# Latent values projected behind the attention's first batch of scores, with the last weight split and the mLSTM tile splits of that place moved to later batches

## The chip, the cores and the metric

The kernel runs on one core of a Trainium2 chip. The time is device microseconds for the whole program. The time before is 1668.84 us, the median of three runs (1668.3 to 1670.27). The profile is of one further execution, which took 1666.45 us.

## The reference

Two layers (DEPTH = 2) of a decoder trunk over 512 tokens of width 1024, float32. Each layer mixes tokens by three head groups fed by one input projection, then does cross-attention into 256 memory tokens and a SwiGLU block, each between RMSNorms. The change is in the token mixing:

```
h = rms_norm(x, norm_mix_pre[l])
(c_q, c_kv, k_rope, ml_q, ..., sw_v) = split(h @ w_in[l])
y_a = mla_mixer(...)          # A: latent attention, 8 heads, causal
y_b = mlstm_mixer(...)        # B: matrix memory, 4 heads, chunks of 128
y_c = dilated_swa_mixer(...)  # C: dilated window attention, 4 heads
y = concatenate([y_a, y_b, y_c]) @ w_out[l]

# inside A:
q  = rms_norm(c_q) @ w_uq     # 8 heads of 64 + 32 (rotary)
kv = rms_norm(c_kv) @ w_ukv   # 8 heads of 64 keys + 64 values
s  = (q . k + q_rope . k_pe) * scale, causal;  out = softmax(s) @ v
```

## The kernel before

**Precision.** Every projection is done as three matmuls on numbers split into a rounded half and a residual: hi*hi, hi*lo, lo*hi (`three`, lines 555 to 557). Weights stream from memory in units of 128 x 1024 floats through a ring of four slots (`RING`). ScalarE makes the rounded half of a unit (`split_unit`, line 990), VectorE the residual (`lo_to`, line 1362), and both calls stand at written places of each engine's program (`split_until(n)`, `lo_until(n)`: make all units below n). A slot is split again once TensorE has used it up (`unit_used`); SyncE loads the next unit once the residual is made (`split_lo`).

**Order.** There is no scheduler: each engine runs a program in a written order and waits for semaphores. ScalarE, VectorE and TensorE each pass through the same numbered steps. `tile_plan` lists the tiles that a projection makes, in the order of use, with the engine that empties each from its bank. In the stretch at hand all go through two banks in turn (`dense`), so a tile waits until the one two places ahead of it has been emptied (`wait_emptied(..., use - 2)`).

**The mLSTM steps.** Nine steps (`ML_STEPS`) work through two head pairs of four key blocks. In step s TensorE makes the scores of block s and the numerators of block s - 1, then a share of the list `BETWEEN` (`do_between`): here 53 items of three matmuls (a few of one): three sliding-window tiles (`sw`) of eight items, four rotations (`rot`), the key (`key`), eight query tiles (`uq`) of two, four key tiles (`uk`) and four value tiles (`uv`). Item i belongs to step i * 9 // 53, so the steps hold 5 or 6 items. ScalarE in step s makes the exponential weights of block s + 1 (`ml_weights`), and on some steps a part of a pair's end: absolute values (`ml_sums`), the reciprocal (`ml_invert`), the rounded output (`ml_output_hi`). VectorE makes the products (`ml_probs`) and on some steps `ml_diagonals`, `ml_denominators`, `ml_finish`, `ml_output_lo`. After that each of the two empties the tiles that the step has completed, and splits the units that are free then. Value tile m is emptied by ScalarE into `v_mla[:, m, :]`. The last step holds k_nope tiles 2 and 3 and the four value tiles; behind it both engines split the unit that takes the value weights' slot (the output projection's fourth).

**The attention batches.** Latent and window heads go in six pairs of three batches (`BATCH`: query blocks 0 and 1, block 2, block 3), 18 in all. At step s TensorE makes the scores of batch s (`pair_scores`), then the output of a pair whose three batches are copied (`pair_out`), then transposes the probabilities of batch s - 2 (`pair_transposes`). VectorE masks and takes the row minimum (`pair_mask`, line 1674) and copies one head's transposes (`pair_copy`, line 1685), ScalarE makes the exponentials (`pair_exp`, line 1245) and copies the other head's (`pair_copy`, line 1234). Even batches have their scores in banks 2 and 3, odd ones in the dense banks, so batch 1 waits for the last value tile to be emptied. Batch s waits for batch s - 2 to be masked. The transposes of batch t wait, for each head, until the copy of batch t - 1 is made. `ml_finish(1)` and `ml_output_lo(1)` of VectorE and `ml_output_hi(1)` of ScalarE stand at batches 0, 1 and 1.

The first output (`pair_out(0)`, line 837) is the first reader of `v_mla`. The output projection starts after the last batch and is the first to read the unit split above.

Of the kernel before, what the change touches and what calls it, by code (L numbers as in the profile page):

```python
# [20 lines left out]
P = 128  # L21
# [89 lines left out]
def tile_plan():  # L111


    plan, uses = {}, []

    def add(name, sub, engine):
        plan.setdefault(name, []).append((len(uses), sub))
        uses.append((sub, engine))

    def whole(name, u0, n, engine="act", order=range(KT)):  # L120
        for m in range(n):
            add(name, [(u0 + m, k * P) for k in order], engine)

    def query(t):

        add("uq", [(U_UQ + t // 4, ((t % 4) * 2 + k) * P) for k in range(2)], "dve" if t % 2 else "act")

    def rotation():
        add("rot", [], "dve")

    whole("in", U_IN, IN_FM, "dve")

    whole("sw", U_SW, 2, "dve")
    rotation()
    whole("sw", U_SW + 2, 1, "dve")
    rotation()
    whole("sw", U_SW + 3, 1, "dve")
    rotation()
    add("key", [], "act")
    query(0)  # L140
    rotation()
    for t in range(1, MLA_HEADS):
        query(t)
    for m in range(4):
        add("uk", [(U_UKV, m * P)], "act")
    for _ in range(TB):
        add("uv", [(U_UKV, SEQ)], "act")
    whole("out", U_OUT, KT, order=OUT_ORDER)
    whole("xk", U_XK, KT)
    whole("xq", U_XQ, KT)  # L150
    whole("xo", U_XO, KT)
    for m in range(KT):
        add("down", [(U_DOWN + (m * FT + k) // KT, (m * FT + k) % KT * P) for k in range(FT)], "act")
    return plan, uses
# [17 lines left out]
def emptied(use):  # L172
# [6 lines left out]
ML_PAIRS = ML_HEADS // 2  # L179
ML_UNITS = ML_PAIRS * TB  # L180
ML_STEPS = ML_UNITS + 1
BETWEEN = [(name, m, k) for use in range(PLAN["sw"][1][0], PLAN["out"][0][0])
           for name in ("sw", "rot", "key", "uq", "uk", "uv") for m, (at, sub) in enumerate(PLAN[name]) if at == use
           for k in range(max(len(sub), 1))]


# [83 lines left out]
def build(nc, x_in, mem_in, w_in, g_in, c_in, out):  # L270
    with ExitStack() as ctx:
# [231 lines left out]
        with nc.Block() as block:  # L503
# [46 lines left out]
            def _(pe):  # L550
                pe.wait_ge(fixed_set, 2)
                for layer in range(DEPTH):
# [134 lines left out]
                    def do_between(step):  # L687

                        for name, m, k in between(step):
                            use = use_of(name, m)  # L690
                            if name == "sw":
                                project_step("sw", m, k, tiles(h_hi), tiles(h_lo))
                            elif name == "uq":
                                if m == 0:
                                    after_norm("q")(k)
                                project_step("uq", m, k, tiles(cq_hi), tiles(cq_lo))
                            elif name == "uk":
                                if m == 0:
                                    after_norm("kv")(k)
                                project_step("uk", m, k, lambda k: ckv_hi[:, :], lambda k: ckv_lo[:, :])  # L700
                            elif name == "uv":
                                s, t = slot(layer, U_UKV), slice(m * P, (m + 1) * P)
                                wait_emptied(pe, layer, use - 2)
                                mm = three(dense[use % 2][:, :], ckv_hi[:, t], ckv_lo[:, t], w_hi[:, s, SEQ:2 * SEQ],
                                           w_lo[:, s, SEQ:2 * SEQ], True, True)
                                mm.then_inc(unit_used if ends_unit(use) else tile_done, 1)
                            elif name == "key":
                                wait_emptied(pe, layer, use - 2)
                                pe.wait_ge(key_scaled, count(key_scaled, layer, 1))
                                pe.matmul(dense[use % 2][:, :], const(C_KEY), c_tile(MISC), start=True, stop=True)\  # L710
                                  .then_inc(tile_done, 1)
                            else:

                                wait_emptied(pe, layer, use - 2)
                                wait_emptied(pe, layer, use_of("sw", m))
                                pe.matmul(dense[use % 2][:, :], const(C_ROT), sw_qk[:, m, :], start=True, stop=True)\
                                  .then_inc(tile_done, 1)
# [45 lines left out]
                    def attention(a, heads, probs, klen, emit_scores, emit_out, before_last):  # L763
# [3 lines left out]
                        for u in range(n_units + LAG + OUT_LAG):  # L767
# [16 lines left out]
                            if w >= 0 and w % TB == TB - 1:  # L784
                                pe.wait_ge(a["copied"], count(a["copied"], layer, w + 1))
                                emit_out(w // TB)

                    def pair_scores(c):

                        for i in range(2):  # L790
                            if c == 0 and i == 0:
                                wait_emptied(pe, layer, use_of("uq", MLA_HEADS - 1))
                                wait_emptied(pe, layer, use_of("uk", 3))
                                pe.wait_ge(ml_prob, count(ml_prob, layer, 2 * ML_UNITS))
                                pe.wait_ge(roped, count(roped, layer, 4))
                            if c == 1 and i == 0:
                                wait_emptied(pe, layer, use_of("uv", TB - 1))
                            if c >= 2:
                                pe.wait_ge(mix_at["masked"], count(mix_at["masked"], layer, batch_end(c - 2, i)))
                        parts = [mix_head(2 * (c // BATCHES) + i)["parts"] for i in range(2)]  # L800
                        last = len(parts[0]) - 1
                        for qb, at, u in batch_blocks(c):
                            n = causal_len(qb)
                            for part in range(last + 1):
                                for i in range(2):
                                    q, k = parts[i][part]
                                    mm = pe.matmul(score_bank(c, i)[:, at:at + n], q[:, qb * P:n], k[:, 0:n],  # L807
                                                   start=(part == 0), stop=(part == last))
                                    if part == last:
                                        mm.then_inc(mix_at["scored"], 1)  # L810
# [53 lines left out]
                    for s in range(PAIR_STEPS + PAIR_LAG + 1):  # L864
                        if s < PAIR_STEPS:
                            pair_scores(s)
                        t = s - PAIR_LAG
                        if t == PAIR_STEPS:
                            for j in range(KT - 2):
                                out_step(0, j)  # L870
                        if t >= 1 and t % BATCHES == 0:
                            pair_out(t // BATCHES - 1)
                        if 0 <= t < PAIR_STEPS:
                            pair_transposes(t)
# [103 lines left out]
            def _(act):  # L978
# [32 lines left out]
                for layer in range(DEPTH):  # L1011
# [144 lines left out]
                    def ml_output_hi(pair):  # L1156
# [3 lines left out]
                        act.activation(h_hi[:, 4 + pair, :], o_gate[:, pair, :], ACT.Copy).then_inc(ml_hi, 1)  # L1160

                    mix_tiles = {"key": lambda m: k_pe[:, :], "uq": lambda m: q_nope[:, m // 2, :],
                                 "uk": lambda m: k_nope[:, m, :], "uv": lambda m: v_mla[:, m, :]}

                    ml_floors(0)
                    ml_weights(0)
# [70 lines left out]
                    def pair_exp(c):  # L1237

                        for qb, at, u0 in batch_blocks(c):
                            n = causal_len(qb)  # L1240
                            for i in range(2):
                                u = u0 + i
                                act.wait_ge(mix_at["masked"], count(mix_at["masked"], layer, u + 1))
                                p = batch_probs(c, i)[:, at:at + n]
                                act.activation(p, p, ACT.Exp, scale=-1.0, bias=stat[:, 0, u:u + 1],  # L1245
                                               accum_out=stat[:, 1, u:u + 1]).then_inc(mix_at["exped"], 1)

                    for s in range(PAIR_STEPS + PAIR_LAG + 1):
                        t = s - PAIR_LAG
# [3 lines left out]
                            pair_copy(t)  # L1253
                        if s < PAIR_STEPS:
                            pair_exp(s)
                        if s == 1:
                            ml_output_hi(1)
                        if t == PAIR_STEPS:
                            pair_hi(MIX_PAIRS - 1)

# [67 lines left out]
            def _(dve):  # L1328
# [57 lines left out]
                for layer in range(DEPTH):  # L1386
# [275 lines left out]
                    def pair_mask(c):  # L1662

                        hd = mix_head(2 * (c // BATCHES))
                        for qb, at, u0 in batch_blocks(c):
                            n = causal_len(qb)
                            for i in range(2):
# [3 lines left out]
                                if 2 * c + i >= PAIR_PROBS and at == 0:  # L1671
# [3 lines left out]
                                    batch_probs(c, i)[:, at:at + n], score_bank(c, i)[:, at:at + n],  # L1675
                                    const(hd["mask"] + SEQ - n, n), -hd["scale"], 3e38, ALU.add, ALU.min,
                                    stat[:, 0, u:u + 1]), mix_at["masked"])

                    def pair_copy(c):

# [6 lines left out]
                    for s in range(PAIR_STEPS + PAIR_LAG + 2):  # L1687
                        if s < PAIR_STEPS:
                            pair_mask(s)
                        if s == 0:  # L1690
                            ml_finish(1)
                        if s == 1:
                            ml_output_lo(1)
                        if 0 <= s - PAIR_LAG < PAIR_STEPS:
                            pair_copy(s - PAIR_LAG)
                        if s >= 1 and s % BATCHES == 0 and s <= PAIR_STEPS:
# [227 lines left out]
```

## Time and profile before

| | |
|---|---|
| median of three runs | 1668.84 us |
| profiled execution, its own time | 1666.45 us |
| its span, first to last instruction | 1664.7 us |
| TensorE busy | 1582.2 us (95%) |
| VectorE busy | 902.6 us (54%) |
| ScalarE busy | 724.4 us (44%) |
| mean granted TensorE clock | 0.996 |

Busy shares are of the span. A matmul's record overlaps the next one's, so TensorE's pace is read from the distance between starts, and its idle time from the brackets behind a row, which give the idle time just before the instruction and what ended it. The mLSTM steps of layer 0 begin near 110 us, the attention batches run from 170.95 to about 243 us; in layer 1 both come some 819 us later. Lines are those of the kernel before.

### The profile page before, as it was taken

What the parts mean: (1) busy time and instruction counts of PE and PEld (TensorE: products, weight loads), DVE (VectorE), ACT (ScalarE), POOL (GpSimd) and SP (SyncE); (2) the same over time, 40 slices, a digit from 0 to 9 for tenths busy, and PEclk for the clock granted to TensorE, in tenths of its full rate; (3) what the DMA queues carried; (4) which work ended last, traced back from release to release, by engine and by line L of the source; (5) the groups of instructions that cost most, each with busy time, mean ns of one, the idle gap of its engine ahead of it and who ended that gap; (6) DMA issues with size and microseconds to landing.
All of it is one profiled execution on the core that took longest, in us unless ns stands there. A gap on an engine that the chain in (4) does not pass through costs nothing.

```text
span 1664.7 us, 19239 instructions
## 1 busy us (share of the span) xinstructions
PE 1582.2 (95%) x7420; PEld 1238.2 (74%) x7420; DVE 902.6 (54%) x1396; ACT 724.4 (44%) x1224; POOL 20.1 (1%) x26
## 2 busy tenths in 40 slices
PE   6999899999999999999989989998999999999995
PEld 5776568777768888888767655787867788888884
DVE  5766645854375555532287666458254655555223
ACT  5544645534444444432245356455254444444221
POOL 0000010000000000000000001000000000000000
PEclk9999999999999999999999999999999999999998
DMA  5321003530212333333212200235302133333321
GB/s 224 108 73 42 1 25 128 165 114 26 89 55 97 102 101 98 99 109 101 89 47 93 89 13 1 89 101 165 101 15 100 51 102 101 102 101 104 111 65 50
DMA packets 38538, 143.47 MB, mean 86 GB/s; under 512 B 4272, under 2 KB 4400, under 8 KB 37936
## 3 DMA queue, kind: packets, MB, share of 16 engines
q1 hardware_dynamic: 38448, 142.25, 26.0%
q8 instruction: 59, 0.97, 0.2%
q14 instruction: 31, 0.25, 0.0%
HBM read 140.13 MB, written 2.10 MB: 85 GB/s over the span
## 4 chain that ended last, share of the span: by engine, by line
PE 87%; DVE 7%; ACT 3%; issue 2%; DMA 0%; SPq 0%; DVEq 0%; ACTq 0%
PE bank L555 25%; PE bank L557 25%; PE bank L556 25%; PE bank L807 2%; PE bank L837 2%; PE bank L915 2%; PE bank L905 1%; PE bank L824 1%; PE bank L747 1%; DVE x L1437 1%; DVE tn_x L1402 1%; PE bank L736 1%; PE bank L602 1%; DVE acc L1343 1%; DVE h_lo L1407 1%
## 5 line engine op out<-in xcount | busy, mean ns | idle before, releaser
L555 PE MATMUL bank<-h_hi,w_hi 128*128 128x512 f32 x1312 | 522.5, 398 | 27.9 <-DVE h_lo L1349 16.8
L1362 DVE TENSOR_TENSOR w_lo<-raw,w_hi 128x1024 fp32r<-128x1024 f32 x254 | 310.2, 1225 | 427.6 <-ACT w_hi L990 425.6
L556 PE MATMUL bank<-h_lo,w_hi 128*128 128x512 f32 x1312 | 512.5, 391 | 0.0
L557 PE MATMUL bank<-h_hi,w_lo 128*128 128x512 f32 x1312 | 512.5, 391 | 0.0
L990 ACT ACTIVATE w_hi<-raw 128x1024 fp32r<-128x1024 f32 x254 | 266.0, 1051 | 186.3 <-PE bank L557 176.0
L555 PEld LDWEIGHTS bank<-h_hi,w_hi 128*128 128x128 f32 x1312 | 247.1, 188 | 97.5 <-issue 25.0
L556 PEld LDWEIGHTS bank<-h_lo,w_hi 128*128 128x128 f32 x1312 | 247.3, 189 | 52.4 <-issue 2.9
L557 PEld LDWEIGHTS bank<-h_hi,w_lo 128*128 128x128 f32 x1312 | 247.1, 188 | 52.5
L556 PE MATMUL bank<-a_lo,w_hi 128*128 128x512 f32 x352 | 136.9, 389 | 0.0
L557 PE MATMUL bank<-a_hi,w_lo 128*128 128x512 f32 x352 | 136.9, 389 | 0.0
L555 PE MATMUL bank<-a_hi,w_hi 128*128 128x512 f32 x352 | 136.9, 389 | 0.0
L1343 DVE TENSOR_TENSOR acc<-acc,sq 128x512 f32<-128x512 f32 x84 | 58.0, 690 | 86.7 <-ACT sq L1009 85.6
L1318 ACT ACTIVATE a_hi<-sq 128x512 fp32r<-128x512 f32 x44 | 27.8, 632 | 140.7 <-DVE sq L1768 140.7
L1009 ACT ACTIVATE sq<-bank 128x512 f32<-128x512 f32 x48 | 28.6, 596 | 125.9 <-PE bank L557 125.9
L556 PEld LDWEIGHTS bank<-a_lo,w_hi 128*128 128x128 f32 x352 | 66.1, 188 | 13.8
L557 PEld LDWEIGHTS bank<-a_hi,w_lo 128*128 128x128 f32 x352 | 66.1, 188 | 13.8
L555 PEld LDWEIGHTS bank<-a_hi,w_hi 128*128 128x128 f32 x352 | 66.1, 188 | 13.5
L1313 ACT ACTIVATE acc<-sq 128x512 f32<-128x512 f32 x44 | 27.8, 632 | 110.0 <-DVE sq L1761 110.0
L555 PE MATMUL bank<-m_hi,w_hi 128*128 128x256 f32 x128 | 38.0, 297 | 5.6 <-DVE w_lo L1362 5.0
L1001 ACT ACTIVATE h_hi<-x,gains 128x512 fp32r<-128x512 f32 x32 | 23.0, 720 | 35.3 <-DVE x L1437 33.2
L1685 DVE COPY pt_mix<-bank 128x384 f32<-128x384 f32 (+1 forms) x36 | 21.7, 601 | 30.9 <-PE bank L824 30.1
L1245 ACT ACTIVATE p_mix<-p_mix,stat 128x128 f32<-128x128 f32 (+2 forms) x72 | 35.7, 499 | 3.9 <-DVE stat L1674 3.9
(210 smaller groups left out, 1850.9 us busy)
## 6 DMA issues: line engine op xcount, KB each, us to landing
raw<-w_in SPq DMA_DIRECT2D x254, 512.0 KB, 3.6
x<-x_in SPq DMA_DIRECT2D x4, 512.0 KB, 8.2
mem<-mem_in SPq DMA_DIRECT2D x2, 1024.0 KB, 4.9
out<-x SPq DMA_DIRECT2D x4, 512.0 KB, 2.6
consts<-c_in SPq DMA_DIRECT2D x1, 1600.0 KB, 12.9
mem_sq<-mem_in SPq DMA_DIRECT2D x1, 1024.0 KB, 6.0
gains<-g_in SPq DMA_DIRECT2D x1, 80.0 KB, 3.4
```

Source lines behind the costliest of these rows:

```text
L555: pe.matmul(out_ap, l_hi, r_hi, start=start, stop=False)
L556: pe.matmul(out_ap, l_hi, r_lo, start=False, stop=False)
L557: return pe.matmul(out_ap, l_lo, r_hi, start=False, stop=stop)
L807: mm = pe.matmul(score_bank(c, i)[:, at:at + n], q[:, qb * P:n], k[:, 0:n], start=(part == 0), stop=(part == last))
L837: mm = pe.matmul(outs[pair % 2][64 * i:64 * i + 64, q0 * P:(q0 + rows.stop - rows.start) * P], mix_head(2 * pair + i)["v"](kb), pt_mix[:, ...
L915: mm = pe.matmul(outs[c][:, :], v_x[:, kb, col:col + P], pt_x[:, head % 2, kb, :], start=(kb == 0), stop=(kb == 1))
L990: act.activation(w_hi[:, s, :], raw[:, s, :], ACT.Copy).then_inc(split_hi, 1)
L1009: act.activation(sq[:, c % 2, 0:width], src, ACT.Square).then_inc(squared, 1)
L1245: act.activation(p, p, ACT.Exp, scale=-1.0, bias=stat[:, 0, u:u + 1], accum_out=stat[:, 1, u:u + 1]).then_inc(mix_at["exped"], 1)
L1313: done(act.activation(sig, gate_up, ACT.Exp, scale=-1.0), act_step)
L1343: ins = dve.tensor_tensor(acc[:, :], acc[:, :], sq[:, c % 2, :], ALU.add)
L1362: dve.tensor_tensor(w_lo[:, s, :], raw[:, s, :], w_hi[:, s, :].bitcast(F32), ALU.subtract)\
```

## The change

The value tiles leave the between list, which now has 49 items over nine steps. TensorE makes them in a new function, `value_tiles`, right behind the scores of batch 0. Tiles 0 and 2 are emptied by ScalarE inside `pair_exp(0)`, tiles 1 and 3 by VectorE inside `pair_mask(0)`, each behind the query block of the same place. Batch 1 waits for tiles 2 and 3. On ScalarE `ml_output_hi(1)` moves from batch 1 to batch 2, and the split of the unit in the value weights' slot to batch 3. On VectorE `ml_output_lo(1)` and the residual of that unit stand at batch 3, between its masks and its copy.

```diff
--- before.py
+++ after.py
@@ -143,8 +143,8 @@
         query(t)
     for m in range(4):
         add("uk", [(U_UKV, m * P)], "act")
-    for _ in range(TB):
-        add("uv", [(U_UKV, SEQ)], "act")
+    for t in range(TB):
+        add("uv", [(U_UKV, SEQ)], "dve" if t % 2 else "act")
     whole("out", U_OUT, KT, order=OUT_ORDER)
     whole("xk", U_XK, KT)
     whole("xq", U_XQ, KT)
@@ -179,8 +179,8 @@
 ML_PAIRS = ML_HEADS // 2
 ML_UNITS = ML_PAIRS * TB
 ML_STEPS = ML_UNITS + 1
-BETWEEN = [(name, m, k) for use in range(PLAN["sw"][1][0], PLAN["out"][0][0])
-           for name in ("sw", "rot", "key", "uq", "uk", "uv") for m, (at, sub) in enumerate(PLAN[name]) if at == use
+BETWEEN = [(name, m, k) for use in range(PLAN["sw"][1][0], PLAN["uv"][0][0])
+           for name in ("sw", "rot", "key", "uq", "uk") for m, (at, sub) in enumerate(PLAN[name]) if at == use
            for k in range(max(len(sub), 1))]
 
 
@@ -698,12 +698,6 @@
                                 if m == 0:
                                     after_norm("kv")(k)
                                 project_step("uk", m, k, lambda k: ckv_hi[:, :], lambda k: ckv_lo[:, :])
-                            elif name == "uv":
-                                s, t = slot(layer, U_UKV), slice(m * P, (m + 1) * P)
-                                wait_emptied(pe, layer, use - 2)
-                                mm = three(dense[use % 2][:, :], ckv_hi[:, t], ckv_lo[:, t], w_hi[:, s, SEQ:2 * SEQ],
-                                           w_lo[:, s, SEQ:2 * SEQ], True, True)
-                                mm.then_inc(unit_used if ends_unit(use) else tile_done, 1)
                             elif name == "key":
                                 wait_emptied(pe, layer, use - 2)
                                 pe.wait_ge(key_scaled, count(key_scaled, layer, 1))
@@ -785,6 +779,16 @@
                                 pe.wait_ge(a["copied"], count(a["copied"], layer, w + 1))
                                 emit_out(w // TB)
 
+                    def value_tiles():
+
+                        s = slot(layer, U_UKV)
+                        for m in range(TB):
+                            use, t = use_of("uv", m), slice(m * P, (m + 1) * P)
+                            wait_emptied(pe, layer, use - 2)
+                            mm = three(dense[use % 2][:, :], ckv_hi[:, t], ckv_lo[:, t], w_hi[:, s, SEQ:2 * SEQ],
+                                       w_lo[:, s, SEQ:2 * SEQ], True, True)
+                            mm.then_inc(unit_used if ends_unit(use) else tile_done, 1)
+
                     def pair_scores(c):
 
                         for i in range(2):
@@ -794,7 +798,8 @@
                                 pe.wait_ge(ml_prob, count(ml_prob, layer, 2 * ML_UNITS))
                                 pe.wait_ge(roped, count(roped, layer, 4))
                             if c == 1 and i == 0:
-                                wait_emptied(pe, layer, use_of("uv", TB - 1))
+                                for m in range(TB - 2, TB):
+                                    wait_emptied(pe, layer, use_of("uv", m))
                             if c >= 2:
                                 pe.wait_ge(mix_at["masked"], count(mix_at["masked"], layer, batch_end(c - 2, i)))
                         parts = [mix_head(2 * (c // BATCHES) + i)["parts"] for i in range(2)]
@@ -864,6 +869,8 @@
                     for s in range(PAIR_STEPS + PAIR_LAG + 1):
                         if s < PAIR_STEPS:
                             pair_scores(s)
+                        if s == 0:
+                            value_tiles()
                         t = s - PAIR_LAG
                         if t == PAIR_STEPS:
                             for j in range(KT - 2):
@@ -1160,7 +1167,7 @@
                         act.activation(h_hi[:, 4 + pair, :], o_gate[:, pair, :], ACT.Copy).then_inc(ml_hi, 1)
 
                     mix_tiles = {"key": lambda m: k_pe[:, :], "uq": lambda m: q_nope[:, m // 2, :],
-                                 "uk": lambda m: k_nope[:, m, :], "uv": lambda m: v_mla[:, m, :]}
+                                 "uk": lambda m: k_nope[:, m, :]}
 
                     ml_floors(0)
                     ml_weights(0)
@@ -1244,6 +1251,8 @@
                                 p = batch_probs(c, i)[:, at:at + n]
                                 act.activation(p, p, ACT.Exp, scale=-1.0, bias=stat[:, 0, u:u + 1],
                                                accum_out=stat[:, 1, u:u + 1]).then_inc(mix_at["exped"], 1)
+                            if c == 0:
+                                empty("uv", 2 * qb, v_mla[:, 2 * qb, :])
 
                     for s in range(PAIR_STEPS + PAIR_LAG + 1):
                         t = s - PAIR_LAG
@@ -1253,8 +1262,10 @@
                             pair_copy(t)
                         if s < PAIR_STEPS:
                             pair_exp(s)
-                        if s == 1:
+                        if s == 2:
                             ml_output_hi(1)
+                        if s == 3:
+                            split_until(U_OUT + RING)
                         if t == PAIR_STEPS:
                             pair_hi(MIX_PAIRS - 1)
 
@@ -1675,6 +1686,10 @@
                                     batch_probs(c, i)[:, at:at + n], score_bank(c, i)[:, at:at + n],
                                     const(hd["mask"] + SEQ - n, n), -hd["scale"], 3e38, ALU.add, ALU.min,
                                     stat[:, 0, u:u + 1]), mix_at["masked"])
+                            if c == 0:
+                                m = 2 * qb + 1
+                                wait_tile(dve, layer, use_of("uv", m))
+                                done(dve.tensor_copy(v_mla[:, m, :], dense[use_of("uv", m) % 2][:, :]), emptied_dve)
 
                     def pair_copy(c):
 
@@ -1689,8 +1704,9 @@
                             pair_mask(s)
                         if s == 0:
                             ml_finish(1)
-                        if s == 1:
+                        if s == 3:
                             ml_output_lo(1)
+                            lo_until(U_OUT + RING)
                         if 0 <= s - PAIR_LAG < PAIR_STEPS:
                             pair_copy(s - PAIR_LAG)
                         if s >= 1 and s % BATCHES == 0 and s <= PAIR_STEPS:
```

## Rows read from the trace of the kernel before

**Rows 1.** The page's chain that ended last, share of the span by engine.

```profile
PE 87%; DVE 7%; ACT 3%; issue 2%; DMA 0%; SPq 0%; DVEq 0%; ACTq 0%
```

**Rows 2.** TensorE's waits, 110 to 190 us: line, releaser, total us, times, longest.

```profile
PE bank L807 <- DVE stat L1674: 2.1, 1, 2.1
PE bank L824 <- DVE pt_mix L1685: 2.0, 1, 2.0
PE bank L555 <- ACT q_nope L1188: 1.5, 1, 1.5
PE bank L710 <- DVE sw_qk L1424: 0.9, 1, 0.9
PE bank L555 <- ACT k_nope L1188: 0.8, 1, 0.8
PE bank L555 <- issue: 0.8, 1, 0.8
```

**Rows 3.** Busy time by engine (PE, PEld, DVE, ACT, POOL), granted clock, DMA: layer 1.

```profile
969.76:1006.86 37.10, 32.22 (x169) 21.25 (x167) 22.41 (x52) 23.11 (x54) 0.00 (x0) 1.00 0.00 1
```

**Rows 4.** TensorE in time order: start us, length us, line, operands, [idle before].

```profile
150.30 0.40 PE L555 MATMUL bank<-cq_hi,w_hi 128*128 128x512 f32 x1
...
150.99 0.39 PE L555 MATMUL bank<-cq_hi,w_hi 128*128 128x512 f32 x1
...
164.85 0.61 PE L747 MATMUL bank<-w_ml,ml_v 128*128 128x128 f32 x4
...
170.95 0.49 PE L807 MATMUL bank<-k_nope,q_nope 64*128 64x128 f32 x4
...
175.87 1.13 PE L807 MATMUL bank<-k_nope,q_nope 64*128 64x512 f32 x4 [2.05 <-DVE stat L1674]
...
177.79 0.87 PE L824 MATMUL bank<-consts,p_mix 128*128 128x128 f32 x6
...
187.52 2.38 PE L837 MATMUL bank<-pt_mix,v_mla 128*64 128x384 f32 x20
```

**Rows 5.** ScalarE in time order, layer 0.

```profile
146.58 0.40 ACT L1133 ACTIVATE w_ml<-sq,acol 128x128 f32<-128x128 f32 x1 [3.94 <-PE bank L747]
...
148.87 0.58 ACT L1188 ACTIVATE q_nope<-bank 128x512 f32<-128x512 f32 x1
...
165.76 1.21 ACT L1146 ACTIVATE conv_in<-bank 64x512 f32<-64x512 f32 x2
...
171.74 1.06 ACT L990 ACTIVATE w_hi<-raw 128x1024 fp32r<-128x1024 f32 x1
...
181.20 0.72 ACT L1245 ACTIVATE tn_mix<-tn_mix,stat 128x512 f32<-128x512 f32 x1 [1.19 <-DVE stat L1674]
...
182.65 0.47 ACT L1234 ACTIVATE pt_mix<-bank 128x384 f32<-128x384 f32 x1
...
184.28 0.49 ACT L1245 ACTIVATE p_mix<-p_mix,stat 128x256 f32<-128x256 f32 x1
```

**Rows 6.** VectorE in time order, layer 0.

```profile
165.62 1.40 DVE L1573 COPY rstd<-bank 64x512 f32<-64x512 f32 x2
...
172.90 1.22 DVE L1362 TENSOR_TENSOR w_lo<-raw,w_hi 128x1024 fp32r<-128x1024 f32 x1 [5.10 <-ACT w_hi L990]
...
175.29 0.42 DVE L1674 CUSTOM_DVE_ANT_0 p_mix<-bank,consts 128x256 f32<-128x256 f32 x1
...
181.93 0.56 DVE L1685 COPY pt_mix<-bank 128x384 f32<-128x384 f32 x1
```

**Rows 7.** TensorE at pauses of the span, and busy time and clock past its end.

```profile
16.53 0.79 PE L555 MATMUL bank<-h_hi,w_hi 128*128 128x512 f32 x1 [2.51 <-DVE w_lo L1362]
...
21.81 0.51 PE L555 MATMUL bank<-h_hi,w_hi 128*128 128x512 f32 x1
...
466.68 0.47 PE L555 MATMUL bank<-h_hi,w_hi 128*128 128x512 f32 x1 [2.14 <-DVE h_lo L1349]
...
1650.00:1655.00 5.00, 0.00 (x0) 0.00 (x0) 3.97 (x7) 0.84 (x2) 0.00 (x0) 0.52 0.00 0
```

## What the change will do to the time: the prediction

> **What bounds the kernel now.** I read the chain of waits first: TensorE carries 87% of the chain that ended last, VectorE 7%, ScalarE 3% [rows 1]. So a change pays only where TensorE stands still. Next I listed TensorE's waits over 110 to 190 us of layer 0, the stretch in which the mLSTM steps with their in-between tiles end and the first attention batches begin. Six pauses matter: 0.9 (for the last sliding-window tile), 0.8 (for the third rotation to be emptied; the view says "issue"), 1.5 (for ScalarE's first query tile), 0.8 (for a k_nope copy), 2.1 (batch 2 of scores waits for batch 0 to be masked) and 2.0 (the second half of the transposes of batch 1 waits for VectorE's copy of batch 0), 8.1 us in all [rows 2]. Layer 1 repeats it: from query 1's second half to the first output 37.1 us, at a granted clock of 1.00 [rows 3], against 187.52 - 150.30 = 37.2 in layer 0 [rows 4]. So one layer is worked out and doubled. No pause outside this stretch is touched.
>
> The unit of measure is one in-between item of three 512-column matmuls: 150.30 to 150.99, 0.69 us [rows 4]. An item behind a pause takes 0.1 longer.
>
> **Part 1, four value items leave the mLSTM steps.** The in-between list shrinks from 53 to 49 items for nine steps, so each boundary slides: eight steps had 47 items ahead of the last, now 43. Nothing is saved by this alone; 4 x 0.69 = 2.75 us stand behind batch 0 instead. What changes is which copy each step waits for. I followed all three engines in their program order, with durations of before.
>
> Removed: key and query 0 now come in step 5, behind numerators 4, not ahead of them. The waits of 0.9 and 0.8 go, because VectorE works off its copy while TensorE does the mLSTM part. Query 1 no longer waits 1.5 for query 0.
> Put in their place: the third sliding-window tile starts on a copy that stands behind VectorE's diagonals (about 0.3 of a wait). In step 5 ScalarE must first make weights 6 and invert pair 0, which took from 146.58 to 148.87, 2.3 us [rows 5]; only then comes the key copy, and rotation 3 waits for it (0.9). Query 3 waits behind `ml_finish(0)` for VectorE's query 1 (0.6). Sum: 1.8 against 3.2, with two fewer restarts. The last step then begins at about 160.05, where it began at 164.85 [rows 4]: 4.8 earlier, of which 2.75 are the items moved, so 2.05 ahead.
>
> In the last step query 7 is now inside it. Its copy on VectorE stands behind the two copies of 1.40 [rows 6] and the maximum (0.7), which needs ScalarE's absolute values of 1.21 [rows 5]. So k_nope 1 starts at 163.5 and waits 0.95. On ScalarE a weight split of 1.06 now stands ahead of the four k_nope copies; they end at 166.75 and TensorE waits another 0.2 and 0.85. Batch 0 starts at 166.8 instead of 170.95 [rows 4], 4.15 earlier, 2.75 of it the moved items: 1.4 ahead. Bounds: if the copies overlap better than I think, the 2.05 stay whole; if the two waits before and the three here each grow by 0.3, nothing is left. I take 1.4.
>
> **Part 2, the values behind batch 0.** Old: batches 0 and 1 took 2.87 us from 170.95, then 2.05 of waiting, because VectorE's residual split (172.90, 1.22) waited for ScalarE's (171.74, 1.06) and the masks stood behind it [rows 4 to 6]. Both splits go to batch 3, so that wait goes. What is late next is the two dense banks. Tiles 2 and 3 need tiles 0 and 1 emptied, and batch 1 needs 2 and 3 emptied. The chain: batch 0 and value tiles 0 and 1 on TensorE, 3.1; VectorE's copy of tile 1, 0.7; two masks of 256 columns at 0.42 and their hand-overs, 0.95 [rows 6]; ScalarE's last exponential, 0.5; its copy of tile 2, 0.6 [rows 5]; hand-overs 0.15. Sum 6.0, so batch 1 starts at 172.8. TensorE has 1.41 + 4 x 0.69 = 4.2 of work in it and waits 1.7 (0.45 ahead of tile 2, 1.2 ahead of batch 1). The copy of a value tile on VectorE is not in the trace; it lies between the 0.56 of a 384-column copy [rows 6] and 0.75, and I take 0.7. Batch 2 follows at 174.3 without a wait, the transposes at 176.2, against 177.79 [rows 4]. Ahead by 1.55: part 2 gives 0.15. That is 2.1 of wait exchanged for 1.7 and restarts.
>
> **Part 3, the late edits.** `ml_output_lo(1)` moves from batch 1 to 3 and its ScalarE half to batch 2. So VectorE's masks of batch 2 and its copy of batch 0 no longer stand behind it, and the 2.0 in front of the batch 1 transposes [rows 2] goes. But the split moved to batch 3 takes its place. VectorE at batch 3 masks, makes `ml_output_lo(1)`, then the residual split, and only then copies the transposes of batch 1, for which the second half of the batch 2 transposes waits. The residual needs ScalarE's half, which stands behind all four exponentials of batch 3. From 176.2: first transposes done and copied, 1.0; two 512-column exponentials, 181.20 to 182.65 before, 1.45; `ml_output_hi(1)`, a 128x512 copy as at 148.87, 0.5; the copy and four exponentials, 182.65 to 184.28 + 0.49 before, 2.1; the split of 1.06; the residual of 1.22 with its hand-over, 1.35; VectorE's copy, 0.56 and 0.15 to TensorE [rows 5, 6]. Sum 8.15: 184.35. TensorE has 5.1 us of work in that time, so it waits 2.9 in one piece. Afterwards 0.5 of transposes and 1.92 of batch 5 (as batch 2, 175.87 to 177.79), so the first output starts at 186.8 against 187.52 [rows 4]. Part 3 costs 0.8: 2.0 of wait becomes 2.9.
> Bounds: if the split's chain were hidden, only the 2.0 would go and this part would gain 2.0; if VectorE is still masking when the split is ready, it costs about 1.5.
>
> From the first output on nothing is queued differently: the ring's last unit is split 11 us later but first used by the output projection, after 235 us. The same bytes move over SP's queue; its load of the next unit hangs on an earlier split. POOL's work is unchanged.
>
> **Sum.** Per layer -1.4 - 0.15 + 0.8 = -0.75; both layers -1.5. The profiled execution took 1666.45 around a span of 1664.7, so 1664.9 by its own time. The median shown is 2.4 higher, so I forecast 1668.84 - 1.5 = 1667.3. A measurement of this kernel can tell about 0.2% (3.3 us) from no change.
>
> **Weighed against the skill.** The new pause of 2.9 is longer than any at the upper level here: 2.14 ahead of 466.68 kept the clock at 1.00, and after the last matmuls it read 0.52 over 1650 to 1655 [rows 7].
> The Trainium skill (TensorE: Matmul & The Clock Gate, HAM oscillation) warns that long enough idle gaps between bursts throttle the array to half, and that this is paid again at each gap; by it each layer could be charged for the pause of part 3, by the row of 466.68 not.
>
> **The rivals.**
> A, the clock falls in the pause of part 3 (the slower side). For it: its length and the thin work on both sides. Against: 2.14 was harmless. Price: at the start of the span a matmul took 0.79 behind a pause at 16.53 and only 0.51 at 21.81, so the array needed 5.3 us of steady work to leave the lower level (half of the upper, 1.2 against 2.4 GHz; the clock column doesn't show this start) [rows 7]. Half of 5.3 is 2.6 per fall. In both layers 1667.3 + 5.3 = 1672.6, in one 1670. It decides if the pause exceeds about 2.5. Chance 0.17, half of it for both layers.
> B, the split's chain is hidden, or VectorE's copy comes before it. For: ScalarE could take the split in a gap if its exponentials waited for masks. Against: VectorE's order is fixed and the copy is written behind the split. Gain 1.4 + 0.15 + 2.0 = 3.55 per layer, 1661.7. Chance 0.10; half way (1664.5) 0.12.
> C, the slid boundaries cost what they save: the waits of steps 5, 6 and 8 are 0.3 longer each. Then part 1 gives 0 and the sum is +1.3: 1670.1. Chance 0.11.
> The forecast has 0.50, its own range 1665.5 to 1669.
>
> **Numbers.** Below 1665.5 lie B, most of its half-way case and a little of the forecast: 0.22. Above 1672.2: A in both layers and the tail of C: 0.14. Within: 0.64. The range leaves out B whole and A in both layers: 1664.0 to 1671.5.
>
> **What would show it.** Right: no wait of 0.9, 0.8 and 1.5 around key and queries; waits of about 1.7 around the value tiles in place of 2.1; one wait of about 2.9 ahead of batch 2's transposes, put down to VectorE's pt_mix copy; value copies half on VectorE at 0.7; the first output 0.75 earlier against the first mLSTM step. Wrong: this last distance is over 1.6 shorter or any longer, the clock is below 1.00 behind the pause, or a wait shows up past 190 us.

## The result, and the profile after

The changed kernel takes 1670.84 us (median of 12 runs, 1669.47 to 1671.81), the kernel before 1667.54 us in 12 runs beside it (1664.68 to 1670.27). The ratio is 1.0021, interval 1.0013 to 1.0029: slower by 3.3 us, where 1.5 us of gain was forecast. The time lies within the stated range of 1664.0 to 1671.5, but the sign is wrong. That the time lies in the range is partly luck: the forecast started from the first three runs of the kernel before (1668.84), and twelve runs put that kernel 1.3 lower. A forecast and a range from there would lie 1.3 lower too, and the time above it.

The shape of the page is unchanged; TensorE carries 87% of the chain as in [rows 1]. TensorE's waits over 110 to 190 us answer to [rows 2]:

```profile
PE bank L829 <- DVE pt_mix L1700: 2.8, 1, 2.8
PE bank L555 <- DVE q_rope L1552: 1.5, 2, 1.0
PE bank L812 <- ACT v_mla L1045: 1.1, 1, 1.1
PE bank L812 <- issue: 0.8, 1, 0.8
PE bank L710 <- ACT k_pe L1195: 0.7, 1, 0.7
PE bank L555 <- DVE sw_qk L1435: 0.4, 1, 0.4
PE bank L555 <- ACT v_mla L1045: 0.2, 1, 0.2
```

The columns are the same: line and releaser, total us, times, longest. The six waits of [rows 2] are gone; the new ones sum to 7.5 us, where there were 8.1 in [rows 2] and one more of 0.2. The largest is one pause of 2.75. TensorE in time order over layer 0 answers to [rows 4] (first row: the first mLSTM scores; then batch 0, the first transposes, the end of the pause, batch 5, the first output, and last the end of the same pause in layer 1):

```profile
109.86 1.13 PE L730 MATMUL bank<-ml_qk 64*128 64x512 f32 x4
...
166.52 0.49 PE L812 MATMUL bank<-k_nope,q_nope 64*128 64x128 f32 x4 [0.81 <-issue]
...
175.88 0.87 PE L829 MATMUL bank<-consts,p_mix 128*128 128x128 f32 x6
...
183.90 1.09 PE L829 MATMUL bank<-consts,tn_mix 128*128 128x128 f32 x4 [2.75 <-DVE pt_mix L1700]
184.92 2.08 PE L812 MATMUL bank<-k_nope,q_nope 64*128 64x512 f32 x4
186.79 1.17 PE L812 MATMUL bank<-k_pe,q_rope 64*128 64x512 f32 x4
187.89 2.38 PE L842 MATMUL bank<-pt_mix,v_mla 128*64 128x384 f32 x20
...
1005.85 0.70 PE L829 MATMUL bank<-consts,tn_mix 128*128 128x128 f32 x4 [2.76 <-DVE pt_mix L1700]
```

The four 512-column matmuls behind the pause have a record of 2.08; the same group took 1.13 at 175.87 in [rows 4]. The reason is in the windows' clock column (behind POOL), for which [rows 3] had 1.00:

```profile
175.00:183.00 8.00, 6.15 (x46) 3.64 (x42) 5.58 (x17) 7.28 (x21) 0.00 (x0) 1.00 0.00 1
183.00:188.00 5.00, 4.10 (x14) 2.01 (x16) 2.70 (x9) 1.31 (x4) 0.00 (x0) 0.66 0.01 3
188.00:193.00 5.00, 5.00 (x56) 3.76 (x58) 2.35 (x6) 1.81 (x5) 0.00 (x0) 1.00 0.00 0
466.00:471.00 5.00, 4.00 (x11) 3.22 (x12) 4.79 (x9) 2.51 (x5) 0.00 (x0) 0.66 0.00 0
...
1006.00:1010.00 4.00, 4.00 (x14) 1.46 (x13) 1.67 (x5) 1.31 (x4) 0.00 (x0) 0.57 0.00 0
1288.00:1293.00 5.00, 3.88 (x10) 3.08 (x11) 4.79 (x9) 2.63 (x5) 0.00 (x0) 0.66 0.00 0
```

The granted clock is at its lower level, 1.2 GHz, for some 3.4 us in both layers: in layer 0 from 183.7, just ahead of the end of the pause, in layer 1 from 1006.3, 0.4 behind its end. It falls at 466 and 1288 us as well, ahead of the feed-forward blocks, where the pause of 2.14 had kept the upper level in [rows 7]. ScalarE and VectorE show what the pause waits for; they answer to [rows 5, 6]:

```profile
180.93 1.04 ACT L997 ACTIVATE w_hi<-raw 128x1024 fp32r<-128x1024 f32 x1
```

```profile
179.90 0.69 DVE L1601 TENSOR_TENSOR h_lo<-o_gate,h_hi 128x512 fp32r<-128x512 f32 x1
182.07 1.23 DVE L1373 TENSOR_TENSOR w_lo<-raw,w_hi 128x1024 fp32r<-128x1024 f32 x1 [1.48 <-ACT w_hi L997]
183.21 0.55 DVE L1700 COPY pt_mix<-bank 128x384 f32<-128x384 f32 x1
```

VectorE stands still for 1.48 until ScalarE has split the unit, makes the residual, and only then copies what TensorE waits for.

Below, distances in us from layer 0's first mLSTM scores (110.75 in the kernel before) carry the comparison; they don't depend on how the span began. The forecast had 56.05, 65.45 and 76.05.

| kernel | batch 0 | first transposes | first output | layer 1's first output | median |
|---|---|---|---|---|---|
| before | 60.20 | 67.04 | 76.77 | 76.66 | 1667.54 |
| after | 56.66 | 66.02 | 78.03 | 78.16 | 1670.84 |

Per layer the stretch grew by 1.26 and 1.50, 2.8 us in all. From layer 0's first output to layer 1's first mLSTM scores the two profiles differ by 1.2 (743.92 against 742.68), and from layer 1's first output to the last matmul by 1.3 (643.94 against 642.63): these are the falls at 466 and 1288, which the profile of the kernel before doesn't have. The first mLSTM scores come 0.9 earlier. Together these are the 4.4 by which the two spans differ (1669.1 and 1664.7).

The mean granted clock of an execution is close to a count of its falls. In the fourteen profiled executions of this document those with 0, 1, 2, 3 and 4 falls ahead of the last matmul have means of 0.996, 0.995, 0.994, 0.993 and 0.992, without an exception. The twelve executions of the changed kernel all have 0.992 or 0.993, so 3 or 4 falls in each. For the kernel before, the means are known in the 60 executions that ran beside the experiments below: 31 have 0.995 or more, 21 have 0.994, 8 have 0.993 or less.

### The profile page after: what moved, and what is told of

The parts are those of the page before. It is cut to its first block, busy times and chain, and to the rows that moved or that the text cites. A ratio compares the mean times of both kernels' runs of the same rounds, so it can differ in the third digit from the quotient of the medians.

```text
span 1669.1 us, 19243 instructions
## 1 busy us (share of the span) xinstructions
PE 1587.4 (95%) x7420; PEld 1241.4 (74%) x7420; DVE 905.4 (54%) x1400; ACT 721.4 (43%) x1220; POOL 20.1 (1%) x26
## 4 chain that ended last, share of the span: by engine, by line
PE 87%; DVE 7%; ACT 3%; issue 2%; DMA 0%; SPq 0%; DVEq 0%; ACTq 0%
PE bank L555 25%; PE bank L557 24%; PE bank L556 24%; PE bank L812 3%; PE bank L842 2%; PE bank L922 2%; PE bank L912 1%; PE bank L829 1%; DVE x L1448 1%; PE bank L741 1%; DVE tn_x L1413 1%; PE bank L602 1%; DVE acc L1354 1%; DVE h_lo L1418 1%; PE bank L730 1%
```

## Experiments

The runs were made in three groups, each with the kernel before beside it. Its medians were 1666.43 (experiments 1, 4, 5 and 3 at batch 4), 1666.55 (2, 6 and the first two kernels of 9) and 1666.59 (3 at batch 3, 7, 8 and the third kernel of 9). The changed kernel itself ran beside 1667.54, 1.1 higher, so against it the ratios to before are compared and not the medians.

**1. The pause filled.** Three extra matmuls with an unused result stand ahead of the second half of batch 2's transposes.

```diff
+                            if c == 2 and i == 1:
+                                keep_busy(3)
                             pe.wait_ge(mix_at["exped"], ...)
```

> The changed kernel with three extra matmuls (0.9 us each, their result is not used) issued in the 2.8 us pause between the two halves of batch 2's transposes. The wait stays as long as it was; only the array is busy in it. Theory 1 (the pause makes the clock fall, and the fall is what made the change slower): no matmuls at the lower level behind it, the first output about 1.6 us earlier in each layer, 1667.6 against 1670.8. Rival (the clock costs nothing here, the change is slower by its waits): 1670.8 or more.

Measured: 1666.1, ratio to before 0.9993 (0.9984 to 1.0002). First output at 76.56 and 76.54: 1.5 and 1.6 earlier than in the changed kernel, though the copy it waits for comes no earlier. Window and rows in layer 0:

```profile
183.00:188.00 5.00, 4.82 (x25) 1.91 (x25) 4.17 (x11) 1.31 (x4) 0.00 (x0) 1.00 0.01 3
```

```profile
181.21 2.74 PE L617 MATMUL bank<-consts 128*128 128x512 f32 x6
184.13 0.63 PE L831 MATMUL bank<-consts,tn_mix 128*128 128x128 f32 x4 [0.18 <-DVE pt_mix L1702]
184.70 1.13 PE L812 MATMUL bank<-k_nope,q_nope 64*128 64x512 f32 x4
```

Only the array's idleness was taken away, and the loss went: from 0.21% above the kernel before to 0.07% below, 4.7 us between the ratios. The two falls are 3.1 of it in the traces. The mean clock shows that the rest need not be the order of work: ten of the eleven executions have 0.995 or 0.996, so at most about one fall each anywhere, and the eleventh, the profiled one, has the two ahead of the feed-forward blocks. Why those became rarer too isn't shown. The fall of the clock is what made the change slower; its rival is refuted.

**2. One matmul instead of three.** The same edit with `keep_busy(1)`.

> The changed kernel with one extra matmul (0.9 us) in the pause ahead of the second half of batch 2's transposes: 1.9 us of pause are left of 2.8, the wait ends when it did. Theory 1: falls become rarer, not impossible (1.96 kept the clock in the kernel before's trace, 1.96 lost it once in the kernel with the split moved alone): 1667 to 1669. Rival (any interruption there lets it fall): 1670 to 1671.

Measured: 1670.95 (1666.59 to 1672.2), ratio 1.0025 (1.0014 to 1.0036). The rival's number: six of seven executions took 1670.63 or more, one 1666.59. So a pause of 1.90 is no safer in the median. But the rival's ground, that any interruption there lets the clock fall, is too strong. The profiled execution has a fall in layer 0 only (first output 77.60) and none in layer 1 (76.49):

```profile
186.00:191.00 5.00, 5.00 (x20) 1.66 (x22) 2.51 (x7) 1.17 (x4) 0.00 (x0) 0.66 0.01 3
1007.00:1012.00 5.00, 4.59 (x32) 2.37 (x34) 3.60 (x11) 1.31 (x4) 0.00 (x0) 1.00 0.01 3
```

The same program loses the clock behind one of two equal pauses. Up to the first output its two layers differ by 1.1; another 0.5 of this fall comes behind it (744.55 to layer 1's first mLSTM scores, against 744.06 in experiment 1, with one fall ahead of the feed-forward block in both).

**3. The residual behind the copy.** VectorE's `lo_until` goes behind `pair_copy`, once at batch 4, once at batch 3.

```diff
                         if s == 3:
                             ml_output_lo(1)
-                            lo_until(U_OUT + RING)
                         if 0 <= s - PAIR_LAG < PAIR_STEPS:
                             pair_copy(s - PAIR_LAG)
+                        if s == 4:      # the other kernel: s == 3
+                            lo_until(U_OUT + RING)
```

At batch 4:

> The changed kernel with one edit: VectorE's residual of the last split stands behind its copy at batch 4 and no longer ahead of the copy at batch 3. Theory 1: the 2.8 pause goes and the clock does not fall: -2.8 and -1.6 us per layer, first output at about 183.5, 1662. Theory without a clock effect: -2.8 per layer, 1665.2. Rival (the value tiles cost): no better than before, 1667.5.

At batch 3:

> The changed kernel with VectorE's copy at batch 3 ahead of the residual of the last split, which stays at batch 3 (so ahead of the masks of batch 4). Theory 1: the pause in batch 2's transposes goes; a shorter one of 1.5 to 1.9 us comes ahead of the first output, because VectorE's masks of batch 4 and its copy of batch 2 now stand behind the residual; first output 75.6 to 76.0 us after the first mLSTM scores against 78.0 and 73.97 (residual at batch 4). 1665 to 1666.5, more if the clock falls there. Rival (only the order against the copy matters): 73.97, 1661.6.

Measured at batch 4: 1661.57, ratio 0.9971 (0.9959 to 0.9982), first output at 73.97 and 73.93, no low clock in either stretch. By the ratios (1.0021 and 0.9971) that is 8.3 us below the changed kernel by this one line's place. The traces give the same: 2.6 per layer are the pause (76.56 to 73.97), 1.5 and 1.6 the clock, 8.3 together. At batch 3: 1665.06, ratio 0.9991 (0.9982 to 1.0), first output at 75.55. The pause moved one consumer on, and at 1.5 us the clock kept its upper level in both layers:

```profile
PE bank L555 <- DVE q_rope L1552: 1.6, 2, 1.0
PE bank L842 <- DVE pt_mix L1700: 1.5, 1, 1.5
```

**4. The split moved alone**, on the kernel before (both engines' split of that unit from behind the value tiles to batch 3, ahead of VectorE's copy).

```diff
-                            if ended(name, m):
+                            if ended(name, m) and name != "uv":
                                 split_until(ended(name, m) + RING)
...
+                        if s == 3:
+                            split_until(U_OUT + RING)
```

> The kernel before with one edit: the last weight split goes from behind the value tiles to batch 3, on both engines, as in the change; value tiles and mLSTM tile splits stay. Theory 1 (the moved residual split in front of VectorE's copy is the cost): the 2.05 wait of batch 2 goes, the 1.96 wait of the batch 1 transposes goes too, a pause of about 2.8 comes ahead of the second half of batch 2's transposes, and the clock falls behind it: first output +2.3 us per layer, 1672. Rival (the value tiles behind batch 0 are the cost): this kernel gains the 2.05 per layer, 1663.5 to 1665.

Measured: 1672.79, ratio 1.0034 (1.0021 to 1.0047). First transposes at 65.61, 1.43 earlier than before; first output at 78.07 and 79.66. So the value tiles aren't needed to make the kernel slower. One step of mine was a miss: the 1.96 wait of batch 1's transposes did not go, since `ml_output_lo(1)` is left at batch 1. In layer 0 the clock fell at this very wait of 1.96, which the kernel before has too, and was low from 178.9 to 182.4. That slowed the work ahead of the next wait, and this wait shrank from 2.53 (layer 1) to 0.94: 1.6 less. So the fall of layer 0 was hidden. In layer 1 the clock kept its level at 1.96 and fell at the pause of 2.53, with only work behind it: 79.66. Layer 1's attention start:

```profile
PE bank L824 <- DVE pt_mix L1687: 4.5, 2, 2.5
PE bank L807 <- DVE stat L1676: 0.6, 1, 0.6
```

**5. The outputs moved alone**, on the kernel before.

```diff
-                        if s == 1:
+                        if s == 2:
                             ml_output_hi(1)
...
-                        if s == 1:
+                        if s == 3:
                             ml_output_lo(1)
```

> The kernel before with one edit: ml_output_hi(1) at batch 2 and ml_output_lo(1) at batch 3, as in the change; values and the split stay. Theory 1: the 1.96 wait ahead of the second half of batch 1's transposes goes, nothing takes its place, the clock stays: -1.8 us per layer, 1663.9. Rival (VectorE's order only shifts the wait to the next batch): 1667.5.

Measured: 1664.95, ratio 0.9992 (0.9983 to 1.0): first output at 75.17 and 74.96, 1.6 and 1.7 earlier, where 1.8 was expected; the medians give 1.5 us of the 3.3, and the interval reaches no change. The mean clock says where the rest may be: all eleven executions have 0.995 or less, 0.994 in eight, and the profiled one has falls at 465 and 1285.

**6. Values between the mLSTM steps again**, with all late edits and the residual at batch 4.

> The previous experiment's late edits (outputs at batches 2 and 3, last split at batch 3 on ScalarE, its residual behind VectorE's copy at batch 4), but on the kernel before: the value tiles stay in the list between the mLSTM steps, all emptied by ScalarE. Theory 1, second part (the value tiles' move is itself worth about nothing): in the trace of the split moved alone batch 2 began 1.5 us earlier in its layer, in the changed kernel with values moved too 1.0 us; so this kernel is 0.4 us per layer faster than the one with values behind batch 0: 1660.7 against 1661.6. Rival (the value tiles behind batch 0 gain, as I forecast: 0.15 to 1.5 us per layer): 1662 to 1664.5.

Measured: 1660.43, ratio 0.9963 (0.9951 to 0.9976). First transposes at 65.59 against 66.05 with the values behind batch 0, first output at 73.65 against 73.97. TensorE's waits:

```profile
PE bank L555 <- ACT q_nope L1188: 1.5, 1, 1.5
PE bank L710 <- DVE sw_qk L1426: 0.9, 1, 0.9
PE bank L555 <- ACT k_nope L1188: 0.8, 1, 0.8
PE bank L555 <- issue: 0.8, 1, 0.8
PE bank L807 <- DVE stat L1676: 0.6, 1, 0.6
```

In the traces moving the values costs 0.5 per layer up to the first transposes and 0.3 up to the first output; the medians (1661.57 and 1660.43) point the same way with overlapping intervals.

**7. Old step boundaries** for the 49 items, with the values behind batch 0 and the residual at batch 4.

```diff
-    return BETWEEN[len(BETWEEN) * step // ML_STEPS:...]
+    n = len(BETWEEN) + TB
+    return BETWEEN[n * step // ML_STEPS:n * (step + 1) // ML_STEPS]
```

> The kernel with the residual at batch 4 and values behind batch 0, but the 49 in-between items keep the step boundaries of the list of 53 (the last step has two items). Theory (the slide of the boundaries gained about 0.9 us per layer, the values behind batch 0 cost more than that): the waits of 0.9, 0.8 and 1.5 around key and queries are back, batch 0 starts 57.5 us after the first mLSTM scores against 56.7; 1663.4. Rival (the slide is worth nothing): 56.7 and 1661.6.

Measured: 1664.52, ratio 0.9987 (0.9978 to 0.9996). Batch 0 at 57.59, first transposes at 66.95, and the waits of 1.5 (q_nope), 0.9 and 0.8 are back:

```profile
PE bank L813 <- issue: 1.5, 1, 1.5
PE bank L556 <- ACT q_nope L1196: 1.5, 1, 1.5
PE bank L813 <- ACT v_mla L1046: 1.0, 1, 1.0
PE bank L705 <- DVE sw_qk L1436: 0.9, 1, 0.9
PE bank L556 <- issue: 0.8, 1, 0.8
```

So the slide gains 0.9 per layer (66.95 to 66.05), and the values behind batch 0 cost 1.35 (65.59 to 66.95 at like boundaries), 1.2 up to the first output (73.65 to 74.87). The median is 3.0 above that of experiment 3, more than the 1.7 of both layers' stretches; the profile here has two falls ahead of the feed-forward blocks, that of experiment 3 one.

**8. All value tiles emptied by ScalarE**, residual at batch 4 (`"dve" if t % 2 else "act"` back to `"act"`, two `empty` calls behind each query block's exponentials, VectorE's two copies out).

> The kernel with the residual at batch 4, but all four value tiles emptied by ScalarE, two behind each query block's exponentials, none by VectorE. Theory: tile 1's copy comes 0.1 to 0.3 later on ScalarE, and ScalarE has two copies of 0.6 ahead of batch 1's start where it had one: +0.5 us per layer at batch 1, 1662.6. Rival (VectorE's copies between its masks are what delays batch 1): earlier by up to 0.7 per layer, 1660.2.

Measured: 1660.88, ratio 0.9966 (0.9953 to 0.9978); first output at 74.07 and 73.73 against 73.97 and 73.93. Neither expectation: who empties them makes no difference that shows.

**9. Six idle matmuls in the old pauses of 2.1**, ahead of the feed-forward blocks and of layer 1 (`keep_busy(4)` to `keep_busy(6)`): on the kernel before, on experiment 3's kernel, and on experiment 6's.

> The kernel before with six instead of four idle matmuls in the three 2.1 us pauses ahead of the feed-forward blocks and the second layer. Theory (part of the spread of the kernel before, 1664.7 to 1670.3, are clock falls in these pauses): median 1 to 1.5 us lower, 1665.3, highest run under 1668. Rival (falls there are rare in the kernel before): 1666.4, spread as it was.

> The changed kernel with the residual behind the copy at batch 4, and six instead of four idle matmuls in each of the three 2.1 us pauses ahead of the feed-forward blocks and the second layer. Theory (these pauses too make the clock fall in some executions, 1.3 us each time, which is why traces and medians differ by more than the waits): no lower level anywhere before the last matmul, 1660.3 to 1661, runs closer together. Rival (the extra matmuls stand in the way or the falls have another cause): 1661.6 or more.

> Values between the mLSTM steps, outputs at batches 2 and 3, the last split at batches 3 and 4, and six idle matmuls in the three 2.1 us pauses. Theory (the two gains add): 1659.2. Rival (the six matmuls gain nothing, as in the kernel before, 1666.1 against 1666.5): 1660.4.

Measured: before 1666.07 (1664.48 to 1671.78), ratio 0.9999 (0.999 to 1.0008); experiment 3's 1660.3, ratio 0.9961 (0.9948 to 0.9973); experiment 6's 1659.92, ratio 0.9959 (0.9945 to 0.9972). The pauses shrink to 0.42 and the profiled executions of all three have no low clock from the first steady work to the last matmul. Yet the medians move by 0.5, 1.3 and 0.5, within the intervals, and the kernel before keeps its spread. The record shows what goes with that spread: nine of its eleven executions have a mean clock of 0.996 and took at most 1666.38, the two longest (1668.84 and 1671.78) have 0.994 and 0.993. The same holds for the 60 executions of the kernel before: the seven above 1667.7 all have 0.993 or less. So the long ones lost the clock more often; where isn't shown, as none of them was profiled. The waits of 2.05 and 1.96 are candidates, since experiment 4 lost it at one of 1.96. The last kernel has the lowest median of all, 6.7 us below the kernel before beside it; its lead over experiments 3, 6 and 8 is not clear of noise.

## Why the prediction was wrong

**Bound and scope: right for the waits.** One stretch, nearly the same in both layers, and no new wait above 0.2 us past the first output. The falls of the clock were not confined to it.

**Part 1: right in kind, 0.6 short in size.** The waits of 0.9, 0.8 and 1.5 went; 0.4, 0.7, 0.5 and 1.0 came where I had 0.3, 0.9, 0.6 and 0.95. Batch 0 came at 56.66 against 56.05 forecast. The working of this part doesn't add up: its own waits, 3.2 + 0.8 before and 1.8 + 0.95 + 0.2 + 0.85 after, leave 0.2 and two restarts of 0.1, not 1.4. Measured, the waits went from 4.2 to 3.5, and the stretch gained 0.8. Most of the missing 0.6 is in the last step: the forecast left 4.75 us of work in it (160.05 to 166.8 less 2.0 of waits), the trace has 5.4 (159.30 to 166.52 less 1.85), and the kernel before had 5.3. The slide gains by itself; experiment 7 sizes it.

**Part 2: right in size, wrong in credit.** From batch 0 to the first transposes I had 9.4, measured 9.36. But I booked the lost split wait (2.1) against the new one (1.7, measured 1.3) as one bargain of +0.15. The experiments separate them: taking the split away is worth 1.4 alone (4; 0.6 of that wait stays), the values behind batch 0 cost 1.35 (6, 7). With the slide's 0.9 the three make 0.95 of the 1.02 that the first transposes moved.

**Part 3: the wait was right.** I had 2.9 of pause and 10.6 from the first transposes to the first output; the trace has 2.75, and 10.50 with the array kept busy (experiment 1). With the clock fallen it is 12.0.

**The step that failed** is the end of part 3: 0.5 for the transposes and 1.92 for batch 5 behind the pause, at the upper level. They took 4.0 where I had 2.4. My ground was the row of 466.68, where 2.14 of pause did no harm [rows 7]. One harmless row was no bound: in the changed kernel that very pause loses the clock too. Over the eleven profiled kernels that have four idle matmuls there, the two pauses of 2.14 ahead of the feed-forward blocks lost it 15 times in 22, and the profile of the kernel before is the only one that lost it at neither. I had the mechanism as rival A, with a chance of 0.17. Its condition, a pause above about 2.5, is refuted: 2.14, 1.96 and 1.90 lost the clock too. With 2.6 per fall its price was too high. I had taken half of the 5.3 us that the array spent at the lower level at the start of the span; a fall in mid-span lasts some 3.4 us, half of that is 1.7, and it measured 1.5 and 1.65 here. Without falls the forecast's sum would have been -0.2 per layer (76.77 to 76.56) instead of -0.75, the 0.6 of part 1 missing. With them it is +1.26 and +1.50; the rest of the 3.3, 0.5, is within the interval (2.2 to 4.8), and falls outside the stretch can make it too, which the forecast had nowhere.

The rule of the Trainium skill (TensorE: Matmul & The Clock Gate, HAM oscillation) that long enough idle gaps between bursts throttle the array, and do so again at each gap, was the better guide here: both layers paid, with 0.66 and 0.57 of the clock in the windows above. Not every gap paid, though: of two equal ones in experiment 2 only one did.

Rival B was the fate of the copy with the order changed: 73.97 in experiment 3, 2.1 less per layer than the forecast's 76.05. Rival C, part 1 giving nothing, did not happen, but part 1 gave 0.8 where the forecast had 1.4.

## What to carry to other kernels

- A late split or copy in front of a copy that the busiest engine waits for costs its own length plus its feeder's whole queue (here 1.23 us of residual and 1.48 of waiting for ScalarE). Place it behind the last short copy of the step, where its engine waits anyway: here one line's place was worth 8 us, the whole change 3.
- Price a new pause of TensorE at the pause plus a fall of the clock, unless many executions show that such a pause keeps it; one row that kept it proves nothing. Look at the mean clock of every execution, not only at the profiled one: here a thousandth of it was one fall. Filling the pause with idle matmuls is a cheap test of which half costs.
- When a change moves several things at once, write each against its own wait. Here the gain of one (the split off the masks' path) hid that another (the values behind batch 0) was a loss.

## What the runs showed of the hardware

Two equal pauses of 1.90 in one execution: behind one the clock fell to half for some 3.4 us, behind the other it stayed (experiment 2). In the eleven profiles of kernels with four idle matmuls in the old pauses, those of 2.14 ahead of the feed-forward blocks lost it in 15 of 22 cases, the one of 2.15 ahead of layer 1 in 1 of 11. So the length of a pause alone doesn't say whether the clock falls.

The low stretch lasted some 3.4 us each time. It began between 0.2 us ahead of the end of the pause (changed kernel, layer 0) and 1.4 us behind it (experiment 6, layer 1, ahead of the feed-forward block: the pause ends at 1280.3, the clock is low from 1281.7).

A fall with no long wait of TensorE behind it cost 1.5 and 1.65 us in the changed kernel's two layers, 1.6 in experiment 2 (1.1 up to the first output and 0.5 behind it), and 1.3 ahead of the feed-forward blocks (743.92 to 744.06 against 742.63 to 742.78 us from layer 0's first output to layer 1's first mLSTM scores). A fall ahead of such a wait cost nothing: in layer 0 of experiment 4 the next wait shrank by 1.6. The one fall ahead of layer 1 (profile of experiment 8) did not lengthen the way to layer 1's first mLSTM scores either (742.67).
